# Gathered rows of two expert tables: ring slots released and refilled row by row, the two tables in turn, instead of four rows at a time

## The chip, the cores and the metric

One Trainium2 chip, one of its cores. The metric is the device time of one execution in microseconds (us), median over the runs; lower is better.

## The reference

One decoder layer over 256 tokens of width 2048, in float32: an input projection, a convolution group and a sparse attention group, an output projection, a layer norm, and then PEER, which is the part that the change touches. Each token picks 16 experts in each of 8 heads (128 experts a token). Each expert is one row of a table U and one row of a table V (16384 x 2048 float32 each).

```python
def block(i):                       # 128 tokens
    ub = u_tab[eb]                  # eb: expert numbers, 128 x 8 x 16
    h = jax.nn.gelu(jnp.einsum('td,thed->the', xb, ub), approximate=False)
    vb = v_tab[eb]
    return jnp.einsum('the,thed->td', gb * h, vb)   # gb: softmax gates
...
x = layer_norm(ALPHA * x + y, ln2_g[l], ln2_b[l])
```

## The kernel before

The 128 partitions hold 128 tokens, and there are two token blocks. For each expert slot (128 a block, 256 in all) one indirect DMA gathers one table row per token: 128 x 2048 float32, 1.049 MB. Such a DMA is called a gather here: u0 to u255 from table U and v0 to v255 from table V, in the order of the slots. Four slots are a group (`G = 4`), 64 groups in all, numbered from 0.

Who does what with them:

- GpSimd (POOL) issues all 512 gathers, in the fixed order of its program (`gather`, L324).
- VectorE (DVE) takes each landed U row: `dots_of` multiplies it with the token block and sums it (L1165), one dot a row. ScalarE turns four dots into four Gelu values. `diags_of` (L1175) then makes for a group four 128 x 128 diagonal matrices of gate times Gelu. Of these there are two sets, so the diagonals of group g wait until TensorE is done with group g - 2 (`y_done`).
- TensorE (PE) adds each landed V row, weighted by its diagonal, into four PSUM banks (`add_rows`, L609). The profile counts 8 matmul records for a gather, two for each bank of 512 columns.
- At every fourth group DVE also picks the experts of the next head (`retrieve`) and handles its gates.

Both tables have a ring of 8 slots in SBUF (`RG = 2` groups of `G`). Gather n of a table can be issued when row n - 8 has been used. The semaphore `dots_done` tells of U rows used, `y_done` of V rows.

The order of GpSimd's program has three stretches. First 40 U gathers (groups 0 to 9) go out, while TensorE still computes the expert queries. Then comes the stretch called CATCH: seven turns, each with two V groups and one U group, in which V catches up (V groups 0 to 13, U groups 10 to 16). Then, to the end, one V group and one U group that is three groups ahead take turns (`LEAD = 3`), and the last three V groups stand alone. GpSimd runs its program in order: while one gather waits for its slot, nothing behind it is issued.

DVE's order in CATCH, turn n: diagonals of groups 2n and 2n + 1, then dots of group 8 + n. After that: diagonals of group g, dots of group g + 1. In the last group pair DVE adds the fourth bank itself, so TensorE has three banks for the last 8 rows. Then come the norm of the second block (`norm_out`) and the output.

Of the kernel before, what the change touches and what calls it, by code (L numbers as in the profile page):

```python
# [22 lines left out]
TI = S // P  # L23
# [11 lines left out]
TOP = 16  # L35
SLOTS = PH * TOP
# [14 lines left out]
G = 4  # L51
RG = 2
GROUPS = SLOTS // G
TURNS = GROUPS // RG

FIRST = 8
CATCH = 7
LEAD = FIRST + RG - CATCH
# [5 lines left out]
def layer(nc, xT, x_tok, w_stream, w_kw, w_sub, conv_p, cln, bucket1h, rel_bias,  # L64
          b_out, ln1_col, ln_rows, u_tab, v_tab, out):
    with ExitStack() as ctx:
# [58 lines left out]
        u_ring = [put(f"u_row{k}", w, [P, D], plus=o) for k, (w, o) in enumerate(u_places)]  # L125
        v_ring = [put(f"v_row{k}", w, [P, D], plus=o) for k, (w, o) in enumerate(v_places)]
# [72 lines left out]
        eid = sb("eid", [P, TI * SLOTS], I32)  # L199
# [43 lines left out]
        gate_sub, gate_exp, picked = sem("gate_sub"), sem("gate_exp"), sem("picked")  # L243
        bank_done = sem("bank_done")
        row2_done, row2_copied = sem("row2_done"), sem("row2_copied")
        u_in = [sem(f"u_in{k}") for k in range(RG * G)]
# [33 lines left out]
        @block.gpsimd  # L280
        def _(pool):
            pool.memset(ident[:, :], 0.0)
            pool.memset(ident_a[:, :], 0.0)
            pool.memset(mean_w[:, :], 1.0 / DC)
            pool.memset(ones_row[:, :], 1.0)
            pool.memset(eps[:, :], EPS)
            pool.iota(iota_i[:, :].rearrange("p (r j) -> p r j", j=TOP), [[0, TOP], [1, TOP]], channel_multiplier=0).then_inc(pool_const, 1)
            pool.wait_ge(pool_const, 1)
            pool.affine_select(out=ident[:, :], in_=ident[:, :], compare_op=ALU.not_equal, fill=1.0,
                               base=0, pattern=[[-1, P]], channel_multiplier=1)  # L290
            pool.affine_select(out=ident_a[:, :], in_=ident_a[:, :], compare_op=ALU.not_equal, fill=ALPHA,
                               base=0, pattern=[[-1, P]], channel_multiplier=1).then_inc(pool_const, 1)
            def cut(ready, ts, fill):

                for i in range(TI):
                    pool.wait_ge(ready, i + 1)
                    pool.affine_select(out=ts[i], in_=ts[i], compare_op=ALU.is_ge, fill=fill,
                                       base=i * P, pattern=[[-1, (i + 1) * P]], channel_multiplier=1).then_inc(causal, 1)


            pool.wait_ge(w_used, U_GLU)
            pool.wait_ge(row_copied, 1)
            pool.dma_start(turned_rows, bass.AP(tensor=dist_row, offset=P - 1, ap=[[SKEW, NH], [-1, P], [1, S]])).then_inc(row_out, 16)
            pool.wait_ge(row_out, 16)
            pool.wait_ge(x_split, 4)
            pool.dma_start(bias, turned_rows.rearrange("h p s -> p h s")).then_inc(bias_in, 16)

            cut(scored, acc, FILL)
            cut(masked, mask, NEG)

            pool.wait_ge(w_used, U_OUT)
            pool.dma_start(b_all, b_out.to_broadcast([P, D])).then_inc(b_in, 16)  # L312
            pool.wait_ge(logit_read, CC)
            pool.dma_start(sub, w_sub).then_inc(sub_in, 16)
            pool.wait_ge(att_turned, CC)
            pool.dma_start(x1, x_tok.rearrange("(i p) d -> p i d", p=P)).then_inc(row_in, 16)

            pool.wait_ge(w_used, U_WQ)
            for k in range(2):
                pool.dma_start(rows[:, k, :], ln_rows[k:k + 1, :].to_broadcast([P, D])).then_inc(row1_in, 16)  # L320

            def gather(tab, dst, ids, land):

                pool.indirect_dma_start(dst, None, tab, bass.IndirectOffsetOnAxis(ap=ids, axis=0)).then_inc(land, 16)  # L324

            def u_group(g):

                if g % (TOP // G) == 0:
                    pool.wait_ge(picked, g // (TOP // G) + 1)
                if g >= RG:  # L330
                    pool.wait_ge(dots_done, g - RG + 1)
                for j in range(G):
                    s = g % RG * G + j
                    gather(u_tab, u_ring[s], eid[:, g * G + j:g * G + j + 1], u_in[s])

            def v_group(g):

                pool.wait_ge(y_done, g + 1)
                for j in range(G):
                    s = g % RG * G + j  # L340
                    gather(v_tab, v_ring[s], eid[:, g * G + j:g * G + j + 1], v_in[s])

            for g in range(FIRST + RG):
                u_group(g)

            pool.wait_ge(w_used, U_END)
            pool.wait_ge(key_copied, 2 + 2 * PH)
            for n in range(CATCH):
                v_group(2 * n)
                v_group(2 * n + 1)  # L350
                u_group(FIRST + RG + n)
            for g in range(2 * CATCH, TI * GROUPS):
                v_group(g)
                if g + LEAD < TI * GROUPS:
                    u_group(g + LEAD)


        @block.tensor
        def _(pe):
# [62 lines left out]
            with pe.Fori(0, CC // 4) as r:  # L422
                for k in range(4):
# [4 lines left out]
                    for half in range(2):  # L428
                        s = 2 * k + half
# [172 lines left out]
            def add_rows(i, r, k, banks):  # L602

                g = r * RG + (k + i * GROUPS)
                pe.wait_ge(diag_done, g + 1)
                for j in range(G):
                    pe.wait_ge(v_in[k * G + j], r * 16 + (16 + 16 * i * TURNS))
                    for n in range(banks):
                        last = pe.matmul(bank(i, n), diag[k][:, j, :], v_ring[k * G + j][:, n * 512:(n + 1) * 512],  # L609
                                         start=False, stop=True, skip_group_check=True)  # L610
                        if banks < 4 and (k, j) == (RG - 1, G - 1):
                            last.then_inc(bank_done, 1)
                if banks == 4:
                    last.then_inc(y_done, 1)

            def residual(i):

# [30 lines left out]
        def _(act):  # L648
# [167 lines left out]
                act.activation(g, g, ACT.Exp).then_inc(gate_exp, 1)  # L816

            def gelu(g):
                act.wait_ge(dots_done, g + 1)
                act.activation(gel[:, g * G:(g + 1) * G], dots[:, g * G:(g + 1) * G], ACT.Gelu).then_inc(gelu_done, 1)  # L820

            def sd_rows(i):
# [19 lines left out]
        def _(dve):  # L842
# [7 lines left out]


            dve.sem_inc(glu_done, 4)
            dve.sem_inc(y_done, RG)
            dve.sem_inc(att_done, 1)
            dve.sem_inc(pv_done, 1)
            for i in range(TI):
# [303 lines left out]
            def dots_of(g):  # L1160

                for j in range(G):
                    s = g % RG * G + j
                    dve.wait_ge(u_in[s], 16 * (g // RG + 1))
                    ins = dve.tensor_tensor_reduce(u_ring[s], u_ring[s], x1[:, g // GROUPS, :], 1.0, 0.0, ALU.mult, ALU.add,  # L1165
                                                   dots[:, g * G + j:g * G + j + 1])
                ins.then_inc(dots_done, 1)

            def diags_of(g):

                dve.wait_ge(gelu_done, g + 1)
                dve.wait_ge(y_done, g + 1)
                for j in range(G):
                    n = g * G + j
                    ins = dve.tensor_scalar(diag[g % RG][:, j, :], ident[:, :], gel[:, n:n + 1],  # L1175
                                            gate[:, g // GROUPS, n % SLOTS:n % SLOTS + 1], ALU.mult, ALU.mult)
                ins.then_inc(diag_done, 1)
# [33 lines left out]
            def norm_out(i):  # L1211

                if i == 0:
                    dve.wait_ge(y_done, RG + GROUPS)
                for n in (3, 0, 1, 2):
                    if i and n < 3:
                        dve.wait_ge(bank_done, n + 1)
                    last = dve.bn_stats(stats[:, n, :], bank(i, n)[:, :])
                link(last)
                dve.bn_aggr(mv[:, i, :], stats[:, 0:4, :]).then_inc(var2, 1)  # L1220
                dve.wait_ge(var2, i + 1)

                res = [x1[:, i, n * 512:(n + 1) * 512] for n in range(4)]
                dve.wait_ge(row2_copied, 8)
                for n in range(4):
                    dve.scalar_tensor_tensor(out=res[n], in0=bank(i, n)[:, :], scalar=mv[:, i, 0:1],
                                             in1=rows[:, 0, n * 512:(n + 1) * 512], op0=ALU.subtract, op1=ALU.mult)
                dve.wait_ge(sd2, i + 1)
                link(dve.reciprocal(rstd[:, i:i + 1], sd[:, i:i + 1]))
                for n in range(4):  # L1230
                    dve.scalar_tensor_tensor(out=res[n], in0=res[n], scalar=rstd[:, i:i + 1],
                                             in1=rows[:, 1, n * 512:(n + 1) * 512], op0=ALU.mult, op1=ALU.add).then_inc(res_done, 1)
# [84 lines left out]
```

## Time and profile before

| | |
|---|---|
| median of 3 runs | 1828.74 us (1826.61 to 1830.51) |
| the profiled execution | 1828.17 us |
| its span, first to last instruction | 1826.0 us |
| TensorE clock granted, mean over the span | 0.919 |
| busy: PE, DVE, POOL, ACT | 1541.4, 1165.0, 719.4, 260.6 us |
| software DMA queue (the gathers) | 547.39 MB, 73.0% of the 16 DMA engines' span |

Lines are written with their start, their duration, the engine, the line of the kernel, the operation, what it writes and reads, how many instructions are merged (x), and in brackets the idle time of the engine ahead of it and what ended it. A buffer's number is left out, so every slot of the ring is `u_row` or `v_row`. A window line gives for each stretch the busy time of each engine, TensorE's granted clock (1.00 is 2.4 GHz, 0.50 is 1.2 GHz), the share of the DMA engines that was busy, and the GB/s moved.

### The profile page before, as it was taken

The numbers are of one execution on the slowest core, as the hardware profiler recorded it, in microseconds if no ns is written. First come the engines' busy times: TensorE is split into PE (matmuls) and PEld (weight loads), VectorE is DVE, ScalarE is ACT, GpSimd is POOL, SyncE is SP. The second block draws the span as 40 slices with busy tenths as digits, with TensorE's granted clock in tenths as the row PEclk, the third lists the DMA queues.
The fourth block names the chain that finished last, engine by engine and source line by source line (L and its number), as shares of the span: only waits on it lengthen the run. The fifth ranks groups of instructions, "written<-read, shape, count | busy, mean of one in ns | idle before, by whom it ended". The sixth has DMA issues, their size and how long they took to land.

```text
span 1826.0 us, 15111 instructions
## 1 busy us (share of the span) xinstructions
PE 1541.4 (84%) x5524; PEld 912.7 (50%) x5524; DVE 1165.0 (64%) x2081; ACT 260.6 (14%) x387; POOL 719.4 (39%) x535
## 2 busy tenths in 40 slices
PE   7979999999998299998978878786778778877877
PEld 6969789977887144443333323332333333333333
DVE  4479999664668625458475675649566574656454
ACT  4423345533011000000100000001000000000000
POOL 0000000000144646456465555545655555465542
PEclk9989999999999599999888988999888888888889
DMA  6664443455599999999999999999999999999995
GB/s 226 149 220 168 177 161 140 160 210 188 197 421 372 423 421 422 422 422 422 422 421 422 422 422 422 421 422 421 423 422 422 422 421 422 421 422 421 422 407 211
DMA packets 90178, 636.90 MB, mean 349 GB/s; under 512 B 10354, under 2 KB 11026, under 8 KB 13586
## 3 DMA queue, kind: packets, MB, share of 16 engines
q0 software_dynamic: 75632, 547.39, 73.0%
q1 hardware_dynamic: 13828, 88.76, 12.8%
q8 instruction: 21, 0.34, 0.1%
q10 hardware_dynamic: 672, 0.21, 0.1%
q14 instruction: 25, 0.20, 0.0%
HBM read 632.12 MB, written 4.19 MB: 348 GB/s over the span
## 4 chain that ended last, share of the span: by engine, by line
PE 38%; DMA 35%; DVE 13%; issue 7%; POOL 4%; ACT 1%; SPq 0%; DVEq 0%; POOLq 0%; ACTq 0%
DMA v_row<-in_v_tab,eid 32%; PE psum L609 27%; POOL u_row L324 4%; DVE scratch L920 4%; DVE w_lo L865 3%; DVE u_row L1165 3%; PE psum L366 3%; PE psum L367 3%; PE psum L368 3%; DMA u_row<-in_u_tab,eid 2%; PE psum L588 1%; PE psum L479 1%; PE psum L636 1%; DMA w_raw<-in_w_stream 1%; POOL v_row L324 0%
## 5 line engine op out<-in xcount | busy, mean ns | idle before, releaser
L609 PE MATMUL psum<-v_row,scratch 128*128 128x512 f32 x2032 | 978.3, 644 | 237.3 <-DMA v_row<-in_v_tab,eid 237.3
L609 PEld LDWEIGHTS psum<-v_row,scratch 128*128 128x128 f32 x2032 | 416.0, 207 | 800.2 <-issue 635.8
L1165 DVE CUSTOM_DVE_ANT_0 u_row<-u_row,x 128x2048 f32<-128x2048 f32 x256 | 572.0, 2284 | 20.7 <-DMA u_row<-in_u_tab,eid 20.4
L324 POOL DMA_INDIRECT v_row<-in_v_tab,eid x256 | 439.3, 1716 | 364.9 <-PE psum L609 284.7
L1175 DVE TENSOR_SCALAR scratch<-ident,gel,gate 128x128 f32<-128x128 f32 x256 | 75.7, 369 | 481.1 <-PE psum L609 459.5
L324 POOL DMA_INDIRECT u_row<-in_u_tab,eid x256 | 271.6, 1061 | 269.4 <-DVE dots L1165 169.2
L366 PE MATMUL psum<-xT_hi,w_hi 128*128 128x256 f32 x640 | 185.5, 290 | 18.2 <-DVE w_lo L865 15.4
L367 PE MATMUL psum<-xT_lo,w_hi 128*128 128x256 f32 x640 | 182.8, 286 | 0.0
L368 PE MATMUL psum<-xT_hi,w_lo 128*128 128x256 f32 x640 | 182.7, 285 | 0.0
L865 DVE TENSOR_TENSOR w_lo<-w_raw,w_hi 128x2048 fp32r<-128x2048 f32 x64 | 146.4, 2289 | 25.5 <-ACT w_hi L669 23.9
L820 ACT ACTIVATE gel<-dots 128x4 f32<-128x4 f32 x64 | 12.6, 204 | 1013.5 <-DVE dots L1165 1013.5
L669 ACT ACTIVATE w_hi<-w_raw 128x2048 fp32r<-128x2048 f32 x64 | 122.4, 1913 | 95.1 <-DMA w_raw<-in_w_stream 95.1
L366 PEld LDWEIGHTS psum<-xT_hi,w_hi 128*128 128x128 f32 x640 | 124.5, 194 | 22.7 <-DVE w_lo L865 15.4
L367 PEld LDWEIGHTS psum<-xT_lo,w_hi 128*128 128x128 f32 x640 | 124.6, 195 | 0.1
L368 PEld LDWEIGHTS psum<-xT_hi,w_lo 128*128 128x128 f32 x640 | 124.5, 195 | 0.0
L588 PE MATMUL psum<-x1T,w_raw 128*128 128x256 f32 x512 | 112.8, 380 | 0.1
L588 PEld LDWEIGHTS psum<-x1T,w_raw 128*128 128x128 f32 x512 | 96.3, 190 | 13.3 <-issue 0.5
L312 POOL DMA_DIRECT2D b_all<-in_b_out x1 | 0.6, 556 | 235.5 <-PE psum L368 235.5
L920 DVE SCALAR_TENSOR_TENSOR scratch<-glu_sb,conv_sb,scratch 128x256 f32<-128x256 f32 x203 | 89.6, 481 | 3.0
L366 PE MATMUL psum<-w_hi,catT_hi 128*128 128x512 f32 x128 | 50.7, 396 | 0.0
L367 PE MATMUL psum<-w_lo,catT_hi 128*128 128x512 f32 x128 | 50.5, 395 | 0.0
L368 PE MATMUL psum<-w_hi,catT_lo 128*128 128x512 f32 x128 | 50.4, 394 | 0.0
(169 smaller groups left out, 808.9 us busy)
## 6 DMA issues: line engine op xcount, KB each, us to landing
w_raw<-in_w_stream SPq DMA_DIRECT2D x80, 1024.0 KB, 4.8
u_row<-in_u_tab,eid POOLq DMA_INDIRECT x256
v_row<-in_v_tab,eid POOLq DMA_INDIRECT x256
xT_raw<-in_xT SPq DMA_DIRECT2D x4, 512.0 KB, 6.8
turned_rows<-dist_row POOLq DMA_DIRECT2D x1, 2048.0 KB, 25.7
bias<-turned_rows POOLq DMA_DIRECT2D x1, 2048.0 KB, 12.1
x<-in_x_tok POOLq DMA_DIRECT2D x1, 2048.0 KB, 9.6
ln_rows_sb<-in_ln_rows POOLq DMA_DIRECT2D x2, 1024.0 KB, 8.2
```

The source lines that it names most:

```text
L324: pool.indirect_dma_start(dst, None, tab, bass.IndirectOffsetOnAxis(ap=ids, axis=0)).then_inc(land, 16)
L366: pe.matmul(dst, a[0], b[0], start=first, stop=False)
L367: pe.matmul(dst, a[0], b[1], start=False, stop=False)
L368: return pe.matmul(dst, a[1], b[0], start=False, stop=last)
L479: last = pe.matmul(ps[6][:, (2 * i + j) * HD:(2 * i + j + 1) * HD], pT[i][:, (j * (i + 1) + b) * P:(j * (i + 1) + b + 1) * P], v_sb[:, b, ...
L588: last = pe.matmul(ps[k % 2][:, 0:S], w[:, c, :], x1T[:, c, :], start=c == 0, stop=c == KC - 1)
L609: last = pe.matmul(bank(i, n), diag[k][:, j, :], v_ring[k * G + j][:, n * 512:(n + 1) * 512], start=False, stop=True, skip_group_check=True)
L669: act.activation(w_hi[k], w_raw[k], ACT.Copy).then_inc(hi_done, 1)
L865: dve.tensor_tensor(w_lo[k], w_raw[k], w_hi[k].bitcast(F32), ALU.subtract).then_inc(lo_dve, 1)
L920: last = dve.scalar_tensor_tensor(out=cacc[t % 2], in0=h[:, t:t + S], scalar=conv_w(c, t), in1=cacc[t % 2], op0=ALU.mult, op1=ALU.add)
L1165: ins = dve.tensor_tensor_reduce(u_ring[s], u_ring[s], x1[:, g // GROUPS, :], 1.0, 0.0, ALU.mult, ALU.add, dots[:, g * G + j:g * G + j + 1])
L1175: ins = dve.tensor_scalar(diag[g % RG][:, j, :], ident[:, :], gel[:, n:n + 1], gate[:, g // GROUPS, n % SLOTS:n % SLOTS + 1], ALU.mult, AL ...
```

## The change

The groups of four go from GpSimd's program. `u_group` and `v_group` become `u_row` and `v_row`, each with one wait and one gather. `dots_done` is raised after each dot and `y_done` after each V row, not after every fourth. A U gather n waits for the dot of row n - 8, a V gather n for the matmuls of row n - 8. The order changes too: in CATCH two V rows and one U row take turns (v0, v1, u40, v2, v3, u41, ...), and behind it one V row and one U row, 12 ahead (v56, u68, v57, u69, ...). The waits of ScalarE and of the diagonals are for whole groups as before. No computation, tile, or amount of data changes. DVE's, TensorE's and ScalarE's orders stay.

```diff
@@ -323,36 +323,34 @@
 
                 pool.indirect_dma_start(dst, None, tab, bass.IndirectOffsetOnAxis(ap=ids, axis=0)).then_inc(land, 16)
 
-            def u_group(g):
-
-                if g % (TOP // G) == 0:
-                    pool.wait_ge(picked, g // (TOP // G) + 1)
-                if g >= RG:
-                    pool.wait_ge(dots_done, g - RG + 1)
-                for j in range(G):
-                    s = g % RG * G + j
-                    gather(u_tab, u_ring[s], eid[:, g * G + j:g * G + j + 1], u_in[s])
-
-            def v_group(g):
-
-                pool.wait_ge(y_done, g + 1)
-                for j in range(G):
-                    s = g % RG * G + j
-                    gather(v_tab, v_ring[s], eid[:, g * G + j:g * G + j + 1], v_in[s])
-
-            for g in range(FIRST + RG):
-                u_group(g)
+            def u_row(n):
+
+                if n % TOP == 0:
+                    pool.wait_ge(picked, n // TOP + 1)
+                if n >= RG * G:
+                    pool.wait_ge(dots_done, n - RG * G + 1)
+                s = n % (RG * G)
+                gather(u_tab, u_ring[s], eid[:, n:n + 1], u_in[s])
+
+            def v_row(n):
+
+                pool.wait_ge(y_done, n + 1)
+                s = n % (RG * G)
+                gather(v_tab, v_ring[s], eid[:, n:n + 1], v_in[s])
+
+            for n in range((FIRST + RG) * G):
+                u_row(n)
 
             pool.wait_ge(w_used, U_END)
             pool.wait_ge(key_copied, 2 + 2 * PH)
-            for n in range(CATCH):
-                v_group(2 * n)
-                v_group(2 * n + 1)
-                u_group(FIRST + RG + n)
-            for g in range(2 * CATCH, TI * GROUPS):
-                v_group(g)
-                if g + LEAD < TI * GROUPS:
-                    u_group(g + LEAD)
+            for n in range(CATCH * G):
+                v_row(2 * n)
+                v_row(2 * n + 1)
+                u_row((FIRST + RG) * G + n)
+            for n in range(2 * CATCH * G, TI * SLOTS):
+                v_row(n)
+                if n + LEAD * G < TI * SLOTS:
+                    u_row(n + LEAD * G)
 
 
         @block.tensor
@@ -610,8 +608,8 @@
                                          start=False, stop=True, skip_group_check=True)
                         if banks < 4 and (k, j) == (RG - 1, G - 1):
                             last.then_inc(bank_done, 1)
-                if banks == 4:
-                    last.then_inc(y_done, 1)
+                    if banks == 4:
+                        last.then_inc(y_done, 1)
 
             def residual(i):
 
@@ -816,7 +814,7 @@
                 act.activation(g, g, ACT.Exp).then_inc(gate_exp, 1)
 
             def gelu(g):
-                act.wait_ge(dots_done, g + 1)
+                act.wait_ge(dots_done, (g + 1) * G)
                 act.activation(gel[:, g * G:(g + 1) * G], dots[:, g * G:(g + 1) * G], ACT.Gelu).then_inc(gelu_done, 1)
 
             def sd_rows(i):
@@ -850,7 +848,7 @@
 
 
             dve.sem_inc(glu_done, 4)
-            dve.sem_inc(y_done, RG)
+            dve.sem_inc(y_done, RG * G)
             dve.sem_inc(att_done, 1)
             dve.sem_inc(pv_done, 1)
             for i in range(TI):
@@ -1164,12 +1162,12 @@
                     dve.wait_ge(u_in[s], 16 * (g // RG + 1))
                     ins = dve.tensor_tensor_reduce(u_ring[s], u_ring[s], x1[:, g // GROUPS, :], 1.0, 0.0, ALU.mult, ALU.add,
                                                    dots[:, g * G + j:g * G + j + 1])
-                ins.then_inc(dots_done, 1)
+                    ins.then_inc(dots_done, 1)
 
             def diags_of(g):
 
                 dve.wait_ge(gelu_done, g + 1)
-                dve.wait_ge(y_done, g + 1)
+                dve.wait_ge(y_done, (g + 1) * G)
                 for j in range(G):
                     n = g * G + j
                     ins = dve.tensor_scalar(diag[g % RG][:, j, :], ident[:, :], gel[:, n:n + 1],
@@ -1211,7 +1209,7 @@
             def norm_out(i):
 
                 if i == 0:
-                    dve.wait_ge(y_done, RG + GROUPS)
+                    dve.wait_ge(y_done, (RG + GROUPS) * G)
                 for n in (3, 0, 1, 2):
                     if i and n < 3:
                         dve.wait_ge(bank_done, n + 1)
```

GpSimd at turn 1 of CATCH, before: gathers v8 to v15 and then u44 to u47 (the slot is the number behind `v_row` or `u_row`).

```order
L324 DMA v_row0_86<-in_v_tab,eid 128x2048 [waits y_done]
L324 DMA v_row1_87<-in_v_tab,eid 128x2048
L324 DMA v_row2_88<-in_v_tab,eid 128x2048
L324 DMA v_row3_89<-in_v_tab,eid 128x2048
L324 DMA v_row4_90<-in_v_tab,eid 128x2048 [waits y_done]
L324 DMA v_row5_91<-in_v_tab,eid 128x2048
L324 DMA v_row6_92<-in_v_tab,eid 128x2048
L324 DMA v_row7_93<-in_v_tab,eid 128x2048
L324 DMA u_row4_82<-in_u_tab,eid 128x2048 [waits dots_done]
L324 DMA u_row5_83<-in_u_tab,eid 128x2048
L324 DMA u_row6_84<-in_u_tab,eid 128x2048
L324 DMA u_row7_85<-in_u_tab,eid 128x2048
```

The same 12 gathers after:

```order
L324 DMA v_row0_86<-in_v_tab,eid 128x2048 [waits y_done]
L324 DMA v_row1_87<-in_v_tab,eid 128x2048 [waits y_done]
L324 DMA u_row4_82<-in_u_tab,eid 128x2048 [waits dots_done]
L324 DMA v_row2_88<-in_v_tab,eid 128x2048 [waits y_done]
L324 DMA v_row3_89<-in_v_tab,eid 128x2048 [waits y_done]
L324 DMA u_row5_83<-in_u_tab,eid 128x2048 [waits dots_done]
L324 DMA v_row4_90<-in_v_tab,eid 128x2048 [waits y_done]
L324 DMA v_row5_91<-in_v_tab,eid 128x2048 [waits y_done]
L324 DMA u_row6_84<-in_u_tab,eid 128x2048 [waits dots_done]
L324 DMA v_row6_92<-in_v_tab,eid 128x2048 [waits y_done]
L324 DMA v_row7_93<-in_v_tab,eid 128x2048 [waits y_done]
L324 DMA u_row7_85<-in_u_tab,eid 128x2048 [waits dots_done]
```

u44 to u47 (slots 4 to 7 of `u_row`) moved up between the V rows, so that v10 and all that follows stand behind u44 and its wait for a dot; each gather has a wait of its own.

GpSimd in the first stretch, before: gathers u24 to u28.

```order
L324 DMA u_row0_78<-in_u_tab,eid 128x2048 [waits dots_done]
L324 DMA u_row1_79<-in_u_tab,eid 128x2048
L324 DMA u_row2_80<-in_u_tab,eid 128x2048
L324 DMA u_row3_81<-in_u_tab,eid 128x2048
L324 DMA u_row4_82<-in_u_tab,eid 128x2048 [waits dots_done]
```

The same after:

```order
L324 DMA u_row0_78<-in_u_tab,eid 128x2048 [waits dots_done]
L324 DMA u_row1_79<-in_u_tab,eid 128x2048 [waits dots_done]
L324 DMA u_row2_80<-in_u_tab,eid 128x2048 [waits dots_done]
L324 DMA u_row3_81<-in_u_tab,eid 128x2048 [waits dots_done]
L324 DMA u_row4_82<-in_u_tab,eid 128x2048 [waits dots_done]
```

The order is the same here; u24 waits for one dot (row 16), where it waited for the last dot of group 4 (row 19).

GpSimd behind CATCH, before: gathers v56 to v59 and u68 to u71.

```order
L324 DMA v_row0_86<-in_v_tab,eid 128x2048 [waits y_done]
L324 DMA v_row1_87<-in_v_tab,eid 128x2048
L324 DMA v_row2_88<-in_v_tab,eid 128x2048
L324 DMA v_row3_89<-in_v_tab,eid 128x2048
L324 DMA u_row4_82<-in_u_tab,eid 128x2048 [waits dots_done]
L324 DMA u_row5_83<-in_u_tab,eid 128x2048
L324 DMA u_row6_84<-in_u_tab,eid 128x2048
L324 DMA u_row7_85<-in_u_tab,eid 128x2048
```

The same after:

```order
L324 DMA v_row0_86<-in_v_tab,eid 128x2048 [waits y_done]
L324 DMA u_row4_82<-in_u_tab,eid 128x2048 [waits dots_done]
L324 DMA v_row1_87<-in_v_tab,eid 128x2048 [waits y_done]
L324 DMA u_row5_83<-in_u_tab,eid 128x2048 [waits dots_done]
L324 DMA v_row2_88<-in_v_tab,eid 128x2048 [waits y_done]
L324 DMA u_row6_84<-in_u_tab,eid 128x2048 [waits dots_done]
L324 DMA v_row3_89<-in_v_tab,eid 128x2048 [waits y_done]
L324 DMA u_row7_85<-in_u_tab,eid 128x2048 [waits dots_done]
```

Here v57 now stands behind u68 and its wait.

## Rows read from the trace of the kernel before

**Rows 1.** The page, 40 slices of 45.65 us: DMA share, GB/s

```profile
DMA  6664443455599999999999999999999999999995
GB/s 226 149 220 168 177 161 140 160 210 188 197 421 372 423 421 422 422 422 422 422 421 422 422 422 422 421 422 421 423 422 422 422 421 422 421 422 421 422 407 211
```

**Rows 2.** Windows, the first stretch and its one stop; columns in the first line

```profile
core 0: us, PE busy (x) PEld busy (x) DVE busy (x) ACT busy (x) POOL busy (x), PEclk, DMA share, GB/s
560.00:576.00 16.00, 16.00 (x80) 14.19 (x79) 15.37 (x45) 1.92 (x5) 3.52 (x4) 1.00 1.02 422
576.00:584.00 8.00, 7.88 (x39) 6.55 (x38) 8.00 (x7) 1.36 (x4) 5.33 (x3) 1.00 0.50 186
```

**Rows 3.** Timeline of DVE around u24's release

```profile
568.86 2.29 DVE L1165 CUSTOM_DVE_ANT_0 u_row<-u_row,x 128x2048 f32<-128x2048 f32 x1
...
579.92 0.08 DVE L1165 DVE_READ_ACCUMULATOR2_ANT dots<- 128x1 f32 x1
```

**Rows 4.** Timeline of POOL: gathers u24, then v8, v12, v14, u44

```profile
578.06 2.74 POOL L324 DMA_INDIRECT u_row<-in_u_tab,eid  x1 [13.63 <-DVE dots L1165]
...
642.78 1.00 POOL L324 DMA_INDIRECT v_row<-in_v_tab,eid  x1 [11.22 <-PE psum L609]
...
656.52 1.00 POOL L324 DMA_INDIRECT v_row<-in_v_tab,eid  x1 [9.01 <-PE psum L609]
...
660.78 1.91 POOL L324 DMA_INDIRECT v_row<-in_v_tab,eid  x1 [0.30 <-issue]
...
666.58 0.94 POOL L324 DMA_INDIRECT u_row<-in_u_tab,eid  x1 [1.68 <-DVE dots L1165]
```

**Rows 5.** Timeline of PE at the first turns of CATCH

```profile
626.64 29.60 PE L609 MATMUL psum<-v_row,scratch 128*128 128x512 f32 x64 [39.85 <-DMA v_row<-in_v_tab,eid]
656.68 27.73 PE L609 MATMUL psum<-v_row,scratch 128*128 128x512 f32 x64 [0.44 <-DMA v_row<-in_v_tab,eid]
686.52 14.00 PE L609 MATMUL psum<-v_row,scratch 128*128 128x512 f32 x32 [2.11 <-DMA v_row<-in_v_tab,eid]
```

**Rows 6.** Timeline of DVE when v7 is done: four diagonals, then dots

```profile
656.36 1.20 DVE L1175 TENSOR_SCALAR scratch<-ident,gel,gate 128x128 f32<-128x128 f32 x4 [12.53 <-PE psum L609]
657.39 2.28 DVE L1165 CUSTOM_DVE_ANT_0 u_row<-u_row,x 128x2048 f32<-128x2048 f32 x1
659.60 0.08 DVE L1165 DVE_READ_ACCUMULATOR2_ANT dots<- 128x1 f32 x1
```

**Rows 7.** Timeline of PE and of DVE's retrieval behind CATCH

```profile
1299.51 15.63 PE L609 MATMUL psum<-v_row,scratch 128*128 128x512 f32 x32 [5.70 <-DMA v_row<-in_v_tab,eid]
...
1740.78 16.86 PE L609 MATMUL psum<-v_row,scratch 128*128 128x512 f32 x32 [3.35 <-DMA v_row<-in_v_tab,eid]
...
1325.13 0.48 DVE L1077 MAX8 val<-scratch 128x8 f32<-128x128 f32 x2
...
1335.14 1.18 DVE L1175 TENSOR_SCALAR scratch<-ident,gel,gate 128x128 f32<-128x128 f32 x4
```

**Rows 8.** Windows of the end (columns as in rows 2)

```profile
1776.00:1782.00 6.00, 1.59 (x3) 0.64 (x3) 5.80 (x9) 0.00 (x0) 3.95 (x2) 0.89 0.63 235
1792.00:1798.00 6.00, 6.00 (x15) 2.66 (x14) 1.69 (x7) 0.00 (x0) 1.26 (x2) 1.00 0.11 45
1798.00:1800.00 2.00, 2.00 (x6) 0.90 (x5) 1.89 (x4) 0.00 (x0) 1.61 (x2) 1.00 0.94 287
1808.00:1810.00 2.00, 2.00 (x6) 0.95 (x5) 0.76 (x1) 0.00 (x0) 0.00 (x0) 1.00 0.54 229
```

**Rows 9.** Timeline of the end: v252's issue, its landing, v255's, TensorE

```profile
1796.44 0.99 POOL L324 DMA_INDIRECT v_row<-in_v_tab,eid  x1 [9.47 <-PE psum L609]
1802.08 0.76 DVE L1247 SCALAR_TENSOR_TENSOR psum<-v_row,weight,psum 128x512 f32<-128x512 f32 x1 [1.38 <-DMA v_row<-in_v_tab,eid]
1810.71 0.76 DVE L1247 SCALAR_TENSOR_TENSOR psum<-v_row,weight,psum 128x512 f32<-128x512 f32 x1 [1.67 <-DMA v_row<-in_v_tab,eid]
1780.50 36.27 PE L609 MATMUL psum<-v_row,scratch 128*128 128x512 f32 x80 [4.41 <-DMA v_row<-in_v_tab,eid]
```

## The prediction

> **What bounds the kernel now.** I read the page's slices first. From slice 11 (502 us) to slice 38 the DMA engines are busy without a break at 421 to 423 GB/s, but for slice 12 (372), 38 (407) and the last (211) [rows 1]. In that time 512 gathers of 1.049 MB run. So a gather costs 1.049 / 0.422 = 2.485 us of DMA, and nothing else sets the middle's pace: v8 starts TensorE at 656.68 and v16 at 686.52 [rows 5], 12 gathers (8 V, 4 U) in 29.84 us, which is 12 x 2.487. TensorE needs 27.73 us for 8 V rows (3.47 each) at 2.4 GHz [rows 5]. The end of the program is therefore: first gather + 512 x 2.485 + **the time in which DMA has nothing queued** + what remains behind the last byte. A change to the order of issue can only act on the last two. So I looked for DMA's gaps next.
>
> There are two now. In the window 576 to 584 DMA moved 186 GB/s: (422 - 186) x 8 / 422 = **4.5 us** idle [rows 2]. The reader is to see that u24 waited for dot 19 (issue at 578.06) although its slot was free from the end of dot 16, 568.86 + 2.21 = 571.07 [rows 3, 4]. Near the end the windows give 187 x 6 / 422 = 2.7, 377 x 6 / 422 = 5.4 and 135 x 2 / 422 = 0.6, together **8.7 us** [rows 8]: the last V groups wait for whole groups of matmuls.
>
> **Edit 1: waits for one row in the first stretch.** u24 goes out at 571.4, not 578.06. From there one gather is released per dot, 2.21 us, which is less than DMA's 2.485, and eight are in flight. The gap closes: **-4.5 us**. Bounds: 0 (if the gather is late for another reason) and -4.5, all of the idle time. The dots behind it follow DMA or DVE, whichever is later; v0 then reaches TensorE about 4.5 us earlier, at 626.64 - 4.5 = 622.1 [rows 5].
>
> **Edit 2: the end.** With rows released one by one, the last twelve V gathers have no gap: v252 needs v244's matmuls, which are done while v246 is moving. But TensorE becomes the limit there. Count from v243's landing: its matmuls end at 3.5; v244 lands two gathers later, at 5.0, and ends at 8.4; v245 to v247 end at 18.8; the last eight take three of four banks, 2.6 each, and end at 39.6. The last byte is 11 gathers behind v244: 5.0 + 27.3 - 1.6 = 30.7. So TensorE ends 8.9 us behind the last byte. Now it ends at 1816.77 [rows 9], and the last byte was at 1808 + 0.54 x 2 = 1809.1 [rows 8]: 7.7. The 1.6 used here is last byte to use, 1810.71 - 1809.1 [rows 9]. Sum: -8.7 + 1.2 = **-7.5 us** (bounds -8.7 and -5).
>
> **Edit 3: the order in CATCH.** This is the costly one. u44 needs the dot of row 36. DVE does it behind the diagonals of group 3, which wait for group 1, that is v7's matmuls. In both kernels u44 goes out after that moment, call it T. But before, v8 to v11 went out earlier (642.78) and v12 on at 656.52, in the moment T [rows 4]. Now only v8 and v9 stand ahead of u44; v10 to v15 stand behind its wait, though the slots of v10 to v14 are free already. The same holds at u48, u52, u56, u60 and u64: **six stops**.
>
> How long is one? v7's matmuls end at 656.24, diagonals start at +0.12, the dot at +1.15, and it ends at +3.36 [rows 5, 6]. GpSimd wakes 0.35 later, in the middle of the next dot. An issue that starts there ends 0.88 behind that dot's end (578.06 + 2.74 = 580.80, dot's end 579.92) [rows 3, 4]: T + 5.57 + 0.88 = T + 6.45. How long until DMA moves again: v252's issue ends at 1797.43 and v255's last byte is at 1809.1 [rows 8, 9], which is four gathers (9.94) and 1.7. **DMA restarts at T + 8.15.** In the next dots GpSimd gets one issue out per 2.21 us [rows 4], still faster than DMA.
>
> From the restart, last bytes fall at 8.15 + k x 2.485, landings 1.6 later. The order u44, v10, v11, u45, v12, v13, u46, v14, v15, u47, v16, v17 gives landings of v10 at 14.7, v11 17.2, v12 22.2, v13 24.7, v14 29.6, v15 32.1, and DMA is empty at 38.0. TensorE, 3.47 a row: v10 ends at 18.2, v11 21.7, v12 25.6, v13 29.1, v14 33.1, v15 36.6. It was idle some 8 us before v10. After idle times of 3.4 to 5.7 us, 32 matmuls took 15.63 to 16.86 where 13.87 (half of 27.73) is full speed [rows 5, 7]: 1.8 to 3.0 more. With 2.0 the chain moves to 20.2, 23.6, 27.1, 30.6, 34.1 and **37.5**. That is the next T. So a turn lasts 37.5 us where DMA needs 29.8: **7.7 us** idle in each of five turns (36.6 to 38.5, so 6.8 to 8.7).
>
> The first stop: v0 starts TensorE at 622.1, eight rows take 29.6 [rows 5], T = 651.7. DMA has from v0's last byte (620.5) 13 gathers more up to v9, empty at 652.8; it restarts at 659.85: 7.1 us. Together 7.1 + 5 x 7.7 = **+45.6 us**.
>
> Here the Trainium skill bears. Its page "DMA: Bandwidth & Descriptors", section on the anatomy of a SWDGE DMA, gives an estimate of 2.0 us fixed plus bytes over 436 GB/s for a DMA issued from GpSimd. The restart row above shows 1.7 + 1.6 = 3.3 us fixed over four gathers. By the page's 2.0 each stop would be 1.3 us shorter, and the total about 8 us lower.
>
> **Edit 4: the order behind CATCH.** v(4g+1) stands behind u(4g+12), which stands behind v(4g-5)'s matmuls. At T the DMA queue still holds the ten gathers issued behind v(4g-5), less what ran while that row landed and was used: 24.9 - 1.6 - 3.5 = 19.8 us. The stop is 8.15 us. Hidden, with 11.6 us to spare. Where DVE retrieves a head, 10.0 us lie between the last dot and the next diagonals [rows 7]; diagonals, dots and retrieval are then 1.2 + 8.8 + 10.0 = 20.0 us, one group's 19.9. Hidden too. Cost 0. If the cover were gone, each of some 48 groups would pay. The first group behind CATCH waits for v51 (23.6 + 8.15 = 31.8 behind the last T) while DMA is busy to 35.5 (u67, v56): no seventh stop.
>
> **Small edits.** One wait per gather: between two issues GpSimd idles 0.30 us already [rows 4], and it is idle more than half of the time; the `y_done` raises ride on matmuls. Cost 0. The other bound: another 0.30 for each of the 384 added waits is 115 us, on an engine that is busy for 719 of 1826 us, so still hidden. DVE's added raises lie on the dots, 8.8 us a group under 19.9 us of DMA.
>
> **Sum** against the profiled execution: 1828.17 - 4.5 - 7.5 + 45.6 = 1861.8. The median is 0.57 above that execution, so **1862 us**, 1.8% slower. About 0.2% (3.7 us) is what a measurement here can tell from no change.
>
> **Rivals.**
> (a) *The queue covers the stops: faster.* If more than 8.15 us (3.3 gathers) were still queued at each T, only edits 1 and 2 would act: 1828.7 - 12.0 = 1817. For it: DMA shows no gap in CATCH now. Against it: at the first T my count leaves 1.1 us, at the others 0.5; and now, at 656.24, v8 is just landing although it was issued at 642.78, with three gathers behind it, of which v10 and v11 will not be there. Chance 0.06.
> (b) *The stops are real but small.* No clock loss (6.8 each) and the first gather's restart: 1797.43 to 1802.08 less 2.485 is 2.2 us fixed, not 3.3 [rows 9], so 5.7 each: 6.0 + 5 x 5.7 = 34.5, and 1851. Chance 0.12.
> (c) *TensorE loses its clock behind CATCH.* V rows now come one per 4.97 us, with 1.5 us of idle between, in place of four and then a pause. A row takes 3.47 us at 2.4 GHz and 6.9 at 1.2 GHz; above 4.97 TensorE is the bound. At half the time in each level a row costs 5.2, 200 rows cost 46 more: 1908. For it: the granted clock does fall after waits of 3.4 us and more [rows 7]. Against it: after 2.11 us of idle 32 matmuls took 14.00 us, near full speed [rows 5]. The skill's page "TensorE: Matmul & The Clock Gate", section on a second failure mode, tells of a kernel whose clock went back and forth through small idle times between matmul groups; by that rule (c) is what comes. Chance 0.05.
> (d) *The stops reach behind CATCH.* If DVE runs late by more than 11.6 us at the retrievals or the first block's norm, the 11 heads left add some us each: 11 x 2 = 22, 1884. Chance 0.07.
> The forecast has 0.70.
>
> **Range.** Forecast's own: 6.8 to 8.7 a turn, end -8.7 to -5, start -4.5 to 0: 1855 to 1873. With (b) the range goes down to 1849. **1849 to 1874**; it leaves out (a), (c), (d). Slower 0.93, same 0.02, faster 0.05.
>
> **What would show it.** In the profile after: DMA flat at 422 from 560 to about 650, no gap at 578; then six gaps of 7 to 8 us, some 37.5 us apart, in each of which GpSimd's `u_row` waits for DVE's dots; none behind about 860; a flat rate up to the last bytes. TensorE's clock near 1.00 behind CATCH. I am wrong if GB/s stay at 422 in CATCH, or if TensorE's idle time behind CATCH goes while the time grows.

## The result: 39.8 us slower

The changed kernel takes 1868.65 us (1867.85 to 1869.8, 4 runs) against 1828.81 us before; the ratio is 1.0214, 95% interval 1.0202 to 1.0226. The forecast was 1862 (1849 to 1874). The profiled execution's span is 1865.7 us against 1826.0, so +39.7.

The page of the changed kernel, 40 slices of 46.64 us (granted clock, DMA share, GB/s), answers to [rows 1]:

```profile
PEclk9989999999998797888899999999999999999999
DMA  5664544455699978888999999999999999999995
GB/s 222 150 213 179 180 156 139 158 214 214 226 422 422 415 298 343 359 349 351 422 407 422 422 421 422 421 421 422 423 422 422 422 422 422 422 422 421 422 422 225
```

The dip at slice 12 is gone, and five slices (14 to 18, 653 to 886 us) fell from 422 to some 340. The rest is flat but for slice 13, in whose last microsecond the first stop begins, and slice 20. So the loss was made in one stretch, CATCH. Windows of it, columns in the first line, answer to [rows 2]:

```profile
core 0: us, PE busy (x) PEld busy (x) DVE busy (x) ACT busy (x) POOL busy (x), PEclk, DMA share, GB/s
560.00:648.00 88.00, 53.41 (x180) 33.54 (x179) 65.33 (x134) 9.96 (x23) 48.74 (x31) 0.81 1.01 422
648.00:666.00 18.00, 11.69 (x27) 4.79 (x26) 9.96 (x12) 0.20 (x1) 9.15 (x6) 0.94 0.64 256
684.00:706.00 22.00, 14.68 (x31) 6.26 (x31) 9.96 (x12) 0.20 (x1) 10.74 (x8) 0.82 0.70 277
722.00:746.00 24.00, 16.79 (x34) 7.12 (x33) 14.45 (x14) 0.20 (x1) 13.42 (x9) 0.79 0.70 269
760.00:784.00 24.00, 16.46 (x34) 6.85 (x33) 18.75 (x52) 1.90 (x4) 13.29 (x10) 0.79 0.74 296
798.00:822.00 24.00, 17.21 (x34) 7.26 (x33) 10.38 (x15) 0.20 (x1) 13.49 (x11) 0.79 0.71 283
834.00:858.00 24.00, 16.23 (x33) 6.71 (x32) 9.96 (x12) 0.20 (x1) 12.02 (x10) 0.80 0.72 278
...
930.00:950.00 20.00, 20.00 (x48) 8.88 (x47) 16.16 (x19) 0.21 (x1) 14.98 (x9) 1.00 0.95 387
950.00:1840.00 890.00, 670.46 (x1441) 262.45 (x1440) 545.12 (x989) 41.20 (x79) 488.15 (x355) 0.99 1.01 422
```

Six stops. The bytes missing against 422 GB/s are 7.1, 7.6, 8.7, 7.2, 7.9 and 8.2 us of DMA. The last two lines show a small dip, 1.7 us, and then 890 us without one.

TensorE's timeline of the changed kernel answers to [rows 5, 7, 9]. The lines start with v0, v10, v18, v26, v34, v42 and v50, then come v72, v240, v243 and v244:

```profile
621.45 37.22 PE L607 MATMUL psum<-v_row,scratch 128*128 128x512 f32 x80 [34.48 <-DMA v_row<-in_v_tab,eid]
664.99 30.59 PE L607 MATMUL psum<-v_row,scratch 128*128 128x512 f32 x64 [6.32 <-DMA v_row<-in_v_tab,eid]
702.89 30.41 PE L607 MATMUL psum<-v_row,scratch 128*128 128x512 f32 x64 [7.32 <-DMA v_row<-in_v_tab,eid]
740.51 30.38 PE L607 MATMUL psum<-v_row,scratch 128*128 128x512 f32 x64 [7.21 <-DMA v_row<-in_v_tab,eid]
778.44 30.19 PE L607 MATMUL psum<-v_row,scratch 128*128 128x512 f32 x64 [7.54 <-DMA v_row<-in_v_tab,eid]
815.41 30.82 PE L607 MATMUL psum<-v_row,scratch 128*128 128x512 f32 x64 [6.79 <-DMA v_row<-in_v_tab,eid]
853.92 26.56 PE L607 MATMUL psum<-v_row,scratch 128*128 128x512 f32 x56 [7.68 <-DMA v_row<-in_v_tab,eid]
...
957.55 3.70 PE L607 MATMUL psum<-v_row,scratch 128*128 128x512 f32 x8 [1.28 <-DMA v_row<-in_v_tab,eid]
...
1801.88 3.70 PE L607 MATMUL psum<-v_row,scratch 128*128 128x512 f32 x8 [1.27 <-DMA v_row<-in_v_tab,eid]
...
1816.82 3.70 PE L607 MATMUL psum<-v_row,scratch 128*128 128x512 f32 x8 [1.27 <-DMA v_row<-in_v_tab,eid]
1821.89 34.57 PE L607 MATMUL psum<-v_row,scratch 128*128 128x512 f32 x80 [1.36 <-DVE scratch L1173]
```

From v10 to v50 each long line begins behind an idle time of 6.3 to 7.7 us that the landing of a V row ended. From 664.99 to 853.92 are five turns, 37.79 us each, where 12 gathers need 29.8.

DVE and GpSimd of the changed kernel at the first stop answer to [rows 4, 6]: the dot of row 36, the next dot, then u44 and v10 on GpSimd.

```profile
652.77 2.28 DVE L1163 CUSTOM_DVE_ANT_0 u_row<-u_row,x 128x2048 f32<-128x2048 f32 x1
654.98 0.08 DVE L1163 DVE_READ_ACCUMULATOR2_ANT dots<- 128x1 f32 x1
...
657.19 0.08 DVE L1163 DVE_READ_ACCUMULATOR2_ANT dots<- 128x1 f32 x1
```

```profile
655.33 2.75 POOL L324 DMA_INDIRECT u_row<-in_u_tab,eid  x1 [23.10 <-DVE dots L1163]
658.38 1.91 POOL L324 DMA_INDIRECT v_row<-in_v_tab,eid  x1 [0.30 <-issue]
```

GpSimd stood 23.1 us in front of u44, with v10 to v15 behind it. It woke 0.35 us after the dot and finished at 658.08, which is 0.89 behind the next dot's end.

**Where the 39.7 us are, by landings.** v0, v72 and v240 have the same number of gathers ahead of them in both kernels (40, 156, 492), so their starts on TensorE can be compared:

| point | before | after | shift | added since the last |
|---|---|---|---|---|
| v0 | 626.64 | 621.45 | -5.2 | -5.2 |
| v72 | 915.29 | 957.55 | +42.3 | +47.5 |
| v240 | 1760.57 | 1801.88 | +41.3 | -1.0 |
| TensorE's end | 1816.77 | 1856.46 | +39.7 | -1.6 |

The 47.5 fall apart into the first stop, 664.99 - 621.45 less 15 gathers (37.3) = 6.3; five turns, 188.9 - 149.1 = 39.8; and v50 to v72, 103.6 less 41 gathers (101.9) = 1.7. (These make 47.8; the kernel before took 0.4 more than its own 116 gathers over the same way.)

The last -1.6 is not the closed gap in DMA. v244 starts 19.9 us behind v240 before and 20.0 after. But the last 80 matmul records, 36.27 us long before, now take 34.57: in front of v244 TensorE had been idle for 1.36 us and not for 4.41, and its clock was granted in full (1.00 over 1820 to 1830 us, against 0.89 over 1776 to 1782 in [rows 8]).

### The profile page after: what moved, and what is told of

It reads as the page before. It is cut to its first block, busy times and chain, and to the rows that moved or that the text cites. A ratio compares the mean times of both kernels' runs of the same rounds, so it can differ in the third digit from the quotient of the medians.

```text
span 1865.7 us, 15111 instructions
## 1 busy us (share of the span) xinstructions
PE 1514.4 (81%) x5524; PEld 879.6 (47%) x5524; DVE 1164.4 (62%) x2081; ACT 260.7 (14%) x387; POOL 712.0 (38%) x535
## 4 chain that ended last, share of the span: by engine, by line
DMA 33%; PE 26%; DVE 16%; POOL 14%; issue 9%; ACT 1%; SPq 0%; DVEq 0%; POOLq 0%; ACTq 0%
DMA v_row<-in_v_tab,eid 30%; PE psum L607 15%; POOL u_row L324 10%; POOL v_row L324 4%; DVE u_row L1163 4%; DVE scratch L918 4%; DVE w_lo L863 3%; DMA u_row<-in_u_tab,eid 3%; PE psum L364 3%; PE psum L366 3%; PE psum L365 3%; DVE scratch L1173 2%; PE psum L586 1%; PE psum L477 1%; PE psum L634 1%
## 5 line engine op out<-in xcount | busy, mean ns | idle before, releaser
L607 PE MATMUL psum<-v_row,scratch 128*128 128x512 f32 x2032 | 949.4, 617 | 305.8 <-DMA v_row<-in_v_tab,eid 281.1
L607 PEld LDWEIGHTS psum<-v_row,scratch 128*128 128x128 f32 x2032 | 381.3, 195 | 874.4 <-issue 421.4
L324 POOL DMA_INDIRECT u_row<-in_u_tab,eid x256 | 396.6, 1549 | 571.7 <-DVE dots L1163 467.2
L1173 DVE TENSOR_SCALAR scratch<-ident,gel,gate 128x128 f32<-128x128 f32 x256 | 71.6, 345 | 522.9 <-PE psum L607 501.1
L324 POOL DMA_INDIRECT v_row<-in_v_tab,eid x256 | 306.9, 1199 | 105.8 <-issue 73.5
L586 PEld LDWEIGHTS psum<-x1T,w_raw 128*128 128x128 f32 x512 | 96.3, 190 | 13.2 <-issue 0.5
L366 PE MATMUL psum<-w_hi,catT_lo 128*128 128x512 f32 x128 | 50.1, 391 | 0.0
## 6 DMA issues: line engine op xcount, KB each, us to landing
u_row<-in_u_tab,eid POOLq DMA_INDIRECT x256, 19.9
v_row<-in_v_tab,eid POOLq DMA_INDIRECT x256, 19.9
```

What stands on the lines that cost most here:

```text
L366: return pe.matmul(dst, a[1], b[0], start=False, stop=last)
L586: last = pe.matmul(ps[k % 2][:, 0:S], w[:, c, :], x1T[:, c, :], start=c == 0, stop=c == KC - 1)
```

## Experiments

The theory of the order: six times in CATCH GpSimd waits in front of a U gather for a dot that VectorE does behind v7's (v15's, ...) matmuls, with free V slots behind the wait, and DMA runs empty. The main rivals: the added waits and increments cost the time, or taking turns between the tables does, wherever it is done.

**e1_old_order.** Single-row release stays, the order goes back to groups:

```diff
-            for n in range(CATCH * G):
-                v_row(2 * n)
-                v_row(2 * n + 1)
-                u_row((FIRST + RG) * G + n)
+            for g in range(CATCH):
+                for n in range(2 * g * G, (2 * g + 2) * G):
+                    v_row(n)
+                for n in range((FIRST + RG + g) * G, (FIRST + RG + g + 1) * G):
+                    u_row(n)
...
```

(and likewise, four and four, behind CATCH).

> The waits and the semaphores for single rows stay; only GpSimd's order goes back to groups (four or eight V gathers, then four U gathers) in CATCH and behind it. Theory of the order (in CATCH v10 to v15 stand behind u44, and u44 behind v7's matmuls and a dot; six such stops): no stop is left, DMA flat from 560 us to the last V gathers, and what single-row release gives at the start (5.2 us by v0's landing in the changed kernel) and at the end (1.6 us) remains: about 1822 us, a little faster than the kernel before. Rival that the added waits and increments cost the time: as slow as the changed kernel, about 1868 us.

Measured: 1825.67 us, ratio to before 0.9979 (0.9970 to 0.9988). The whole loss is gone with the order alone, so the waits are innocent. The gain is 3.4 us by the medians (the kernel before took 1829.11 in these rounds), half of what was expected.

**e2_catch_old.** Only CATCH goes back to groups; behind it the tables take turns as in the change (the first half of the diff above).

> As the changed kernel, but CATCH alone issues in groups of eight V and four U gathers; behind CATCH one V and one U gather still take turns. Theory of the order: the six stops go, the stretch behind CATCH costs nothing (the U gather's wait is hidden by ten queued gathers): 1822 to 1825 us. Rival that taking turns between the two tables itself slows DMA or GpSimd: most of the loss stays, since 400 of the 512 gathers still take turns, about 1860 us.

Measured: 1824.75 us, ratio 0.9983 (0.9973 to 0.9992). That is as fast as e1, so taking turns costs nothing net where the U gather's wait is covered. In detail it loses a little in one dip (340 GB/s over 880 to 900 us, where e1 has none) and gains 1.7 us in the last 80 matmul records (34.57 us, where e1 takes 36.27).

**e3_catch_new.** The reverse: the changed CATCH, groups behind it.

> As the changed kernel in CATCH (two V gathers, one U gather in turn, with its six stops), but behind CATCH gathers go in groups of four again, released one by one. Theory of the order: all of the loss is made in CATCH: 1868 us, as the changed kernel. Rival that the two stretches share the loss: about 1850 us or less.

Measured: 1870.33 us, ratio 1.0229 (1.0214 to 1.0245), as the changed kernel (1.0214). Its windows, CATCH and the long stretch behind it:

```profile
640.00:860.00 220.00, 176.00 (x372) 75.65 (x371) 79.06 (x138) 4.01 (x9) 89.08 (x70) 0.88 0.83 331
950.00:1750.00 800.00, 634.13 (x1279) 267.53 (x1278) 499.26 (x926) 39.09 (x74) 447.70 (x323) 0.88 1.01 422
```

**e4_dve_swap.** GpSimd keeps the changed order; VectorE's order in CATCH changes:

```diff
                 next_diags(2 * n)
-                next_diags(2 * n + 1)
                 dots_and_next(FIRST + n)
+                next_diags(2 * n + 1)
```

> As the changed kernel, GpSimd's order untouched; in CATCH VectorE does the dots of group 8 + n between the diagonals of group 2n and those of 2n + 1, so that u44's dot waits for v3's matmuls and no longer for v7's. At that moment nine gathers are queued (about 17 us of DMA) against a chain of 8 us. Theory of the order: no stops, 1822 to 1828 us. Rival that taking turns between tables, or GpSimd's slower issues during the dots, cost the time: no change, about 1868 us.

Measured: 1824.35 us, ratio 0.9974 (0.9963 to 0.9985). Its window of CATCH, and u44's issue:

```profile
640.00:880.00 240.00, 220.93 (x493) 91.21 (x492) 119.16 (x220) 8.32 (x17) 126.29 (x95) 0.99 1.01 422
```

```profile
644.31 2.74 POOL L324 DMA_INDIRECT u_row<-in_u_tab,eid  x1 [9.38 <-DVE dots L1163]
```

u44 goes out 11.0 us earlier than in the changed kernel, and 13.2 us earlier when both are counted from v0's start (623.59 here). GpSimd still waits 9.4 us in front of it, but DMA stays at 422 GB/s: by my estimate (v0's last byte at 622.0, then 13 gathers) the queue lasts to 654.3, and u44's issue ends at 647.05. This is the cleanest proof: same order of gathers, same waits, and the loss is gone. What mattered was which matmuls stood ahead of the dot.

**e5_group_waits.** The changed order, with one wait per group (and the semaphores raised once per group, as in the kernel before):

```diff
-                if n >= RG * G:
-                    pool.wait_ge(dots_done, n - RG * G + 1)
+                if n >= RG * G and n % G == 0:
+                    pool.wait_ge(dots_done, n // G - RG + 1)
...
-                pool.wait_ge(y_done, n + 1)
+                if n % G == 0:
+                    pool.wait_ge(y_done, n // G + 1)
```

> The changed kernel's order of gathers with the waits and semaphores of the kernel before, one per group. u44 now waits for the last dot of group 9, which ends at T + 10.0, not T + 3.4, with no dot running then: DMA would restart at T + 10.35 + 0.94 + 1.7 = 13.0, not 8.15. Theory of the order: each of the six stops grows by 4.9 us, 29 in all, and the gains at the start and the end go (5.2 and 1.6): about 1904 us; behind CATCH the longer wait (13.0) is still under the 19.8 us queued. Rival that the single-row waits are what costs: faster than 1868 us.

Measured: 1911.32 us, ratio 1.0456 (1.0437 to 1.0476). The first and the last turn's start on TensorE (v10 and v50), and u44's issue:

```profile
675.87 29.50 PE L608 MATMUL psum<-v_row,scratch 128*128 128x512 f32 x64 [12.02 <-DMA v_row<-in_v_tab,eid]
...
888.02 12.15 PE L608 MATMUL psum<-v_row,scratch 128*128 128x512 f32 x21 [12.08 <-DMA v_row<-in_v_tab,eid]
```

```profile
666.74 0.94 POOL L324 DMA_INDIRECT u_row<-in_u_tab,eid  x1 [21.77 <-DVE dots L1164]
```

A turn lasts (888.02 - 675.87) / 5 = 42.43 us, 4.6 more than in the changed kernel; 4.9 were expected. With no dot running the issue takes 0.94 us. The total came out 7 us above the forecast: this kernel's page has two slices below 422 right behind CATCH (408 and 355, together 9 us of DMA), so there the longer wait was not all hidden, as I had taken it to be. Most of it (273 GB/s over 960 to 980 us) comes behind the norm rows, where GpSimd waits 23.1 us for a dot.

**e6_dot_rows and e7_y_rows.** The kernel before, its order kept, with one half of the release each. e6:

```diff
-                if g >= RG:
-                    pool.wait_ge(dots_done, g - RG + 1)
                 for j in range(G):
+                    if g >= RG:
+                        pool.wait_ge(dots_done, (g - RG) * G + j + 1)
...
-                ins.then_inc(dots_done, 1)
+                    ins.then_inc(dots_done, 1)
```

e7 does the same with `y_done` (`pool.wait_ge(y_done, g * G + j + 1)` ahead of each V gather, an increment for each row).

> The kernel before, its order of gathers untouched, with one part of the change: the dots release U slots one by one (V slots still by groups). Only the start can gain: u24 goes out behind dot 16 and not dot 19, so v0 reaches TensorE at about 621.5 and not 626.6, and all of the 5.2 us last to the end: 1824 us. Rival that the start's gain is lost again in CATCH because TensorE, not DMA, sets its pace: 1828 to 1829 us.

> The kernel before, its order untouched, with the other part: TensorE releases V slots one by one (U slots still by groups). Only the end can gain. The prediction took 8.7 us of idle DMA there for lost time and so 7.5 us of gain: 1821.5 us. Read again by landings, v240 to v255 now take 50.1 us for 19 gathers that need 47.2, so that only 2.9 us are lost, and TensorE sets the end anyway: 1.6 us of gain, 1827.5 us.

Measured: e6 1825.21 us, ratio 0.9982 (0.9973 to 0.9991); e7 1829.41 us, ratio 1.0003 (0.9994 to 1.0012). So the start's gain is real (3.5 us by the medians, 1828.71 against 1825.21), and all of e1's gain. The end's gain cannot be measured. e7's rows at the end: the window in which DMA had stopped before, a window behind its last stretch at full rate, TensorE from v244 on, and VectorE at v255's landing:

```profile
1776.00:1782.00 6.00, 2.90 (x5) 1.18 (x4) 5.32 (x7) 0.00 (x0) 0.99 (x1) 0.77 1.02 423
1803.00:1807.00 4.00, 4.00 (x11) 1.77 (x10) 1.30 (x2) 0.00 (x0) 0.00 (x0) 1.00 0.06 27
```

```profile
1779.66 36.02 PE L609 MATMUL psum<-v_row,scratch 128*128 128x512 f32 x80 [3.10 <-DMA v_row<-in_v_tab,eid]
```

```profile
1807.71 0.76 DVE L1247 SCALAR_TENSOR_TENSOR psum<-v_row,weight,psum 128x512 f32<-128x512 f32 x1 [1.69 <-DMA v_row<-in_v_tab,eid]
```

The gap at 1776 to 1782 is closed (423 GB/s against 235 in [rows 8]), and v255 lands 3.0 us earlier. But TensorE still needs 36 us from v244 on. It ends 1.1 us earlier than in [rows 9], and 0.8 of that it already had at v244's start. A gap was filled that cost next to nothing.

**e10, e8, e9: TensorE out of the end.** For the last eight rows VectorE adds two banks, TensorE two:

```diff
-                add_rows(1, TURNS - 1, k, 3)
+                add_rows(1, TURNS - 1, k, 2)
...
+                for b in (3, 2):
+                    last = dve.scalar_tensor_tensor(out=bank(1, b)[:, :], in0=v_ring[s][:, b * 512:(b + 1) * 512],
...
```

e10 is the kernel before with this, e8 is e1 with it, e9 is e2 with it.

> The kernel before, and nothing of the change. For the last eight rows VectorE adds two of the four PSUM banks and TensorE only the other two (3 each before: TensorE three, VectorE one). Theory that TensorE sets the end (it finishes 6.1 us behind the last landing): it now ends 1.7 us behind v255's landing at 1810.7, so 4.4 us are gained: 1824.5 us. Rival that DMA sets the end: no gain, 1829 us.

> e1 (single-row release, the order of the kernel before) with VectorE adding two banks for the last eight rows. Single-row release lands v255 some 3 us earlier than the kernel before does, counted from v244; while TensorE sets the end that is worth little (e7 gained nothing that can be measured). Theory: with TensorE out of the way it becomes visible: 6.5 us under e1, about 1819 us. Rival that the end is set elsewhere: as e1, 1825 us.

> e2 (groups in CATCH, one V and one U gather in turn behind it, single-row release) with VectorE adding two banks for the last eight rows. In e2 TensorE starts v244 on time and at full clock, so the end gains what lies between the last landing and TensorE's end, some 5 us: about 1819 us, within 2 us of e8. This would be the fastest of the kernels. Rival: as e2, 1825 us.

Measured: e10 1825.99 us, ratio 0.9986 (0.9977 to 0.9995), 2.8 us where 4.4 were expected. e8 1820.83 us, ratio 0.9958 (0.9945 to 0.9972). e9 1821.34 us, ratio 0.9957 (0.9944 to 0.9971). e8's end, v255 on VectorE and on TensorE:

```profile
1804.01 1.41 DVE L1249 SCALAR_TENSOR_TENSOR psum<-v_row,weight,psum 128x512 f32<-128x512 f32 x2 [0.72 <-DMA v_row<-in_v_tab,eid]
```

```profile
1803.96 1.99 PE L610 MATMUL psum<-v_row,scratch 128*128 128x512 f32 x4 [0.18 <-DMA v_row<-in_v_tab,eid]
```

VectorE right behind its last add:

```profile
1805.45 2.49 DVE L1219 BATCH_NORM_STATS2 stats<-psum 128x6 f32<-128x512 f32 x4
```

Both engines now end within 2 us of the last landing. e8 and e9 beat the kernel before by 0.4%, the best of this study. Against e1 e8 gains 4.8 us by the medians where 6.5 were expected; e9 gains 3.4 against e2 where some 5 were. What the forecasts left out is VectorE's norm: with the adds on VectorE all four of the norm's bank statistics (2.49 us) stand behind the last add, where in e1 three of the four are done before TensorE ends. From the last add or matmul to the end of the span it is 12.0 us in e8 and 11.9 in e10, against 9.2 in e1 and in the kernel before.

## Why the prediction was right, point by point

- **What bounds the kernel.** Right. DMA's pace per gather set the middle in every kernel, and each stop lasted to the end: v72 is 42.3 us late, v240 41.3.
- **Edit 1, the start.** Forecast -4.5, measured -5.2 at v0. v0 was forecast at 622.1 and came at 621.45. Other traces differ by some 2 us: v0 starts at 618.8 to 623.6 (mean 621.3) in the eight kernels whose dots release single rows, and at 624.9 to 627.3 (mean 626.2) in the four others, 4.9 apart. e6 keeps 3.5 of it by the medians; where the rest goes no run shows.
- **Edit 2, the end.** This term was mis-sized: -7.5 forecast, -1.6 measured (-0.2 in e7's trace from v240 on, nothing in its time). The half on the changed kernel held: from v243's start to TensorE's end 39.6 us were forecast, and 1856.46 - 1816.82 = 39.6 came. The half on the kernel before failed: I took 8.7 us of missing bytes there for lost time. By landings v240 to v255 took 1810.71 - 1760.57 = 50.1 us where 19 gathers need 47.2, so only 2.9 were lost; the changed kernel took 47.2. TensorE's lag behind v255's landing grew from 6.1 to 7.4, by 1.3 where 1.2 had been forecast. So it was the -8.7 that failed: it came to -2.9. And TensorE, not DMA, set the end: e1 lands v255 47.7 us behind v240 and still ends 56.3 behind it, as the kernel before (56.2). The changed kernel ends 54.6 behind it, because its last 80 matmul records ran at the full clock (34.57 us, not 36.27), a gain for which the forecast had no term.
- **Edit 3, CATCH.** Right in place, number and mechanism. That the size came out so close was in part luck. First T forecast 651.7; the diagonals behind it start at 651.74. End of u44's issue forecast T + 6.45 = 658.1, measured 658.08. From T to T a turn took 37.5 us on average, as forecast (37.79 by the starts from v10 to v50), but two errors cancel in it. The first V row behind a stop reached TensorE 13.4 to 14.9 us behind T (mean 14.1), not 14.7: from the end of the U issue to that row, less two gathers, it was 1.9 to 3.5 us (mean of six stops 2.7), where 3.3 had been assumed. And from that row to the next T it was 23.5 us, not 22.8, because the lower clock cost 2.7 us a turn (30.4 against 27.7 for eight rows), not 2.0. First stop 7.1 against 6.3, sum 45.6 against 46.1. e1, e2, e3 and e4 show the cause, e5 its price.
- **Edit 4, behind CATCH.** Right for the ordinary groups: -1.0 us from v72 to v240. One wait was missed. Between v50 and v72 1.7 us were lost that I had at 0, and the changed kernel's trace shows the chain (GpSimd in front of a U gather, then VectorE):

```profile
932.58 2.24 POOL L324 DMA_INDIRECT u_row<-in_u_tab,eid  x1 [18.53 <-DVE dots L1163]
```

```profile
928.48 1.12 DVE L1173 TENSOR_SCALAR scratch<-ident,gel,gate 128x128 f32<-128x128 f32 x4 [21.44 <-ACT gel L818]
```

  At 915 to 926 us TensorE prepares the norm rows, ScalarE copies them, and its next Gelu stands behind the copies in ScalarE's own order. VectorE's diagonals wait for that Gelu, the dots stand behind the diagonals, and GpSimd waits for a dot, with V gathers behind it: the same stop as in CATCH, once, and DMA falls to 357 GB/s at 930 to 940. e2 and e4 have the same wait (19.9 and 21.4 us) and dip to 340 and 318 GB/s over 880 to 900. From v0 to v72 they take 2.2 and 2.9 us more than e1, which waits 15.7 us there without a dip. By their medians they are no slower than e1; 1.7 us of the loss comes back at the end, where their last 80 matmul records take 34.57 us and e1's 36.27.
- **Rivals.** (a) fell: from 652.0 to 658.6 DMA moved 22 GB/s. (b) fell as a whole, for a turn was 37.8 us and not 35.5; but the restart was half-way to it (2.7 us between its 2.2 and the forecast's 3.3), and the clock loss that it left out made up for that. (c) fell, and the other way: behind CATCH the granted clock rose from 0.88 to 0.99. (d) fell but for the 1.7 us, which came at the norm as it says.

The sum with the measured terms: -5.2 + 6.3 + 39.8 + 1.7 - 1.0 - 1.6 = 40.0, against 39.7 measured. The forecast's 33.6 was short by the end's 5.9 and little else.

## What to carry to other kernels

When one engine issues for two rings in program order, the order is a chain: put a wait in front of a gather only if enough transfers are queued to cover everything that must happen before it is met. Count every engine in that chain, and what each does in its own order before it gets there, as ScalarE's copies here. In CATCH the forecast had 8.15 us against 0.5 us queued, and some 8 us of DMA went missing at each stop; with the same waits and the other order, or with the dot moved ahead of the diagonals, it was covered. Finer release is worth only what was idle on the path: 3.5 us at the start, nothing at the end while TensorE sets it. With TensorE out of the way it is worth some 1.7 there (e8 against e10 is 5.2 us, less the 3.5 of the start). Value a gap by when its transfers land and who uses them last, not by missing bytes.

## What the hardware showed that I had not expected

**One DMA engine runs behind the other fifteen.** The changed kernel's last window before v255 lands:

```profile
1842.00:1848.00 6.00, 6.00 (x15) 2.66 (x14) 1.98 (x3) 0.00 (x0) 0.00 (x0) 1.00 0.06 27
```

The profile gives only the mean over the 16 engines, so what follows is read from it. A share of 0.06 is one engine of 16, and 27 GB/s is a sixteenth of 422. At that rate a sixteenth of a row gather (1.049 MB / 16) takes 2.4 us, and v252 to v255 landed 2.46 us apart (1841.71, 1844.17, 1846.63 and 1849.09 on VectorE). So for 6 us one engine alone was still moving its part of the last rows, and they landed at its pace. e7's window above shows it too, and so does the gap in [rows 8] (0.11 over 1792 to 1798, and 0.06 over its part from 1794 to 1796). The others' idle time is no measure of loss while that one works.

**Small idle times did not cost TensorE its clock.** With 1.27 us of idle in front of each row, the granted clock was 0.99 over 890 us; with some 4 us in front of four rows [rows 7] it was 0.88 over 950 to 1750 us in the kernel before, and the same in e3. The Trainium skill, page "TensorE: Matmul & The Clock Gate", section on a second failure mode, tells of a kernel whose clock went back and forth through small idle times between matmul groups; at 1.27 us in front of 3.70 us of matmuls these runs do not show that.

**An issue on GpSimd takes longer while VectorE runs a dot.** u44's issue took 2.75 us when it began in the middle of a dot, and ended 0.89 behind that dot's end; in e5, with no dot running, it took 0.94. At the six stops it took 2.23 to 2.75 us, so this made up 1.3 to 1.8 of each stop's 8 us.
